# Sample state updates of a Gated DeltaNet kernel as rounded products on 96 stacked rows

## The chip, the cores and the metric

The kernel runs on one NeuronCore of a Trainium2 chip. The metric is the device time in microseconds of one launch, as the median of the runs. The matmul engine is called PE here, with PEld for its weight loads; DVE is the vector engine, ACT the scalar engine, POOL is GpSimd, SP issues the loads of the weights.

## The reference, cut to what matters

One inference step of one decoder layer: 256 prompt tokens and 8 sample sequences of 8 new tokens each (64 sample tokens), an input projection, eight MoBA attention heads, eight Gated DeltaNet heads, an output projection and a convolutional FFN. The change touches the last line of the delta rule, for the samples only:

```
def step(s, xs):
    ...
    u = lax.linalg.triangular_solve(lower, rhs, left_side=True, lower=True, unit_diagonal=True)
    qk = jnp.einsum('bhid,bhjd->bhij', qc, kc) * decay
    o = eg[..., None] * jnp.einsum('bhcd,bhde->bhce', qc, s) + jnp.einsum('bhij,bhje->bhie', qk, u)
    g_last = cg[..., -1]
    k_dec = kc * jnp.exp(g_last[..., None] - cg)[..., None]
    s_new = jnp.exp(g_last)[..., None, None] * s + jnp.einsum('bhcd,bhce->bhde', k_dec, u)
```

For a sample the chunk is its 8 tokens, so `s_new` of one sequence and one head is a 128x128 state plus a product over 8 rows: keys `k_dec` (8x128) against update rows `u` (8x128). There are 8 sequences and 8 heads.

## The kernel before

**Chunks.** All dense products stream their weights in chunks of 512x256 values (512 KB). The first 144 chunks (`NC1`) are the input projection (g0 and g1, the two groups of four DeltaNet heads, 32 chunks each; a0 and a1, the attention groups, 24 each) and the output projection; the FFN follows. For each chunk SP loads `w_raw`, ACT writes its rounded part `w_hi` (L821), DVE the rest `w_lo` (L1173), and PE runs 24 matmuls of 320 columns (L1774 to L1776: high by high, high by low, low by high). These products take fp32r operands, that is rounded ones, and are called rounded products here. The ring has four slots. PE waits at the head of chunk c for `w_lo` of chunk c (`products`). In chunk c ACT makes the high part of chunk c+3 first, DVE the low part of chunk c+2 first, and then each serves its other steps. DVE also takes the finished columns of every fourth chunk out of PSUM (`evac`) and, for g0 and g1, runs four taps of the convolution in the two chunks behind that (`conv`, L1223 and L1225: at quarter 1 and quarter 3 of each).

**Steps.** Everything else of the mixer is cut into steps, and `schedule()` lays them into the quarters of the chunks: `SLOTS[c, r]` is the list of steps behind quarter r of chunk c. PE serves its steps of a quarter behind that quarter's six matmuls; ACT and POOL serve all steps of a chunk in their order behind the chunk's first duty; DVE does, with the taps behind the steps of their quarter. Each engine works strictly in that order. `schedule()` counts in its own units: a step on PE moves the count `at` on by its `LENGTH` times 0.85 times `SPREAD`; a step elsewhere moves the due time `ready` of the next PE step by its `LENGTH` times `SPREAD` (1.4 for the delta rule). So the LENGTH of a step on ACT or DVE delays every later step of the chain.

**The sample unit.** `gdn_steps(g)` has units u = 0, 1 (prompt) and 2 (the 64 sample tokens). For unit 2: `kk` and `kq` (products of keys and queries), `tk` (PE turns the keys to token rows, DVE scales them into `tok_k`), `pl` and `dx` at levels 2 and 4 (the block inverse), `sh` (the state seen by keys and queries), `ks`, `u` (the update rows, ACT copies them to `u_tok`), `os`, `o`, `oc`, `oq`, `o1`, `or`, `o2`, `ot`, `oz` (the output). `ot` of the unit before sits behind `pl` at level 2, its `oz` on DVE behind that, and `sh` of head 0 waits for this `oz`. Then four times, once for each head: `um` (DVE, L1168 inside the helper: the 64 update rows times a mask, spread over four sequences, into `u_mask`), `us` on PE (L2057) and `us` on DVE (the decayed old state, then the sum, two operations on 128x1024), `so` (POOL stores the state). `um` 1 to 3 wait for the PE step `us` of the head before; `us` on PE waits for its `um`; `ot` waits for `o2` and for the last `us` on DVE.

PE's `us` before is two ordinary fp32 products, sequences 0 to 3 on rows 0 to 31 and sequences 4 to 7 on rows 32 to 63:

```
for i in range(2):
    ins = pe.matmul(psB[:, h % 2 * 2 + i, :], tk[32 * i:32 * i + 32, STATE_HEADS[h], :],
                    umask[32 * i:32 * i + 32, :, :].rearrange("p b e -> p (b e)"), start=True, stop=True)
```

**Where the steps lie before** (chunk, quarter). Group 0: `tk`, `pl` 2, `ot` of unit 1 at 40.2; `dx` 2 at 40.3; `sh` 0, `tv`, `pl` 4 at 41.1; `sh` 1, `dx` 4 at 41.3; `sh` 2, `sh` 3, `ks` at 42.1; `u` at 42.3; `os`, `o`, `oc`, `um` 0, `o1` at 43.0; `us` 0 to 3 at 44.0, 45.1, 46.2, 47.3; `ot` at 48.3. Group 1: `tk` and what follows at 72.3, `us` 0 to 3 at 76.1, 77.2, 78.3, 80.0; `ot` at 81.0.

Of the kernel before, what the change touches and what calls it, by code (L numbers as in the profile page):

```python
# [17 lines left out]
F32 = mybir.dt.float32  # L18
F32R = mybir.dt.float32r
I32 = mybir.dt.int32  # L20
ACT = mybir.ActivationFunctionType
ALU = mybir.AluOpType
AX = mybir.AxisListType

P = 128
# [3 lines left out]
NS = DB * DT  # L29
# [14 lines left out]
BLK = 32  # L44
# [133 lines left out]
STATE_HEADS = (1, 2, 3, 0)  # L178
# [7 lines left out]
def gdn_steps(g):  # L186
    decay = decay_steps((g, 0))
    s = decay[:1] + [("A", "qs", g, 0), ("P", "nr", g, 0), ("V", "ss", g, 0), ("G", "rn", g, 0)] + decay[1:]
    tail = []
    for u in (0, 1, 2):  # L190
        k, nxt = (g, u), (g, u + 1)
# [13 lines left out]
        s += tail[:1] + [("P", "tk", *k), ("V", "tk", *k)]  # L205
# [27 lines left out]
        s += [("P", "u", *k), ("A", "u", *k), ("P", "os", *k), ("A", "o", *k)]  # L233
# [9 lines left out]
        tail = [("V", "o2", *k), ("P", "ot", *k), ("V", "oz", *k)]  # L243
# [48 lines left out]
def ffn_param_steps():  # L292
    s = []
    for r in range(5):
# [156 lines left out]
def build(nc, I, O):  # L451
# [37 lines left out]
    work_at = m.at  # L489
    qn = m.put("q_squares", [P, 4, P])  # L490
    kb_at = m.at
    kb = m.put("k_squares", [P, 4, P])
    setat = m.at
# [3 lines left out]
    bv = m.put("tok_bv", [P, 4, P])  # L497
    qk = m.put("qk_t", [P, 4, P])
# [23 lines left out]
    umask = nc.alloc_sbuf_tensor_at("u_mask", [P, 4, P], F32, offset=setat + 4 * 2048)  # L522
# [64 lines left out]
    def C(name, n=P, m_=None):  # L587
        at, width = CONST_COLS[name]
        return cst[0:n, at:at + (width if m_ is None else m_)]
# [21 lines left out]
    def over_free(ap, count):  # L611

        return ap.unsqueeze(2).broadcast_to([ap.shape[0], ap.shape[1], count])

    def over_heads(ap, count):

        return ap.unsqueeze(1).broadcast_to([ap.shape[0], count, ap.shape[1]])
# [47 lines left out]
    def after(e, *key):  # L665

        e.wait_ge(done[key[0]], TALLY[key])
# [24 lines left out]
    root1 = cst[:, CONST_COLS["bucket"][0]:CONST_COLS["bucket"][0] + TOK]  # L692

# [43 lines left out]
    with block:  # L737
# [74 lines left out]
        def _(act):  # L812
            def finish(ins):
                ins.then_inc(done["A"], 1)
# [30 lines left out]
            def step(x):  # L845
# [74 lines left out]
                elif name == "u":  # L920
                    n = unit(k[1])[0]
                    after(act, "P", "u", *k)
                    finish(act.activation(ub[0:n].rearrange("p h d -> p (h d)"), b1[0:n], ACT.Copy))
                elif name == "o":
# [235 lines left out]
        def _(dve):  # L1160
            def finish(ins):
                ins.then_inc(done["V"], 1)
# [4 lines left out]
            def tt(out, a_, b_, op):  # L1167
                return dve.tensor_tensor(out, a_, b_, op)  # L1168
# [82 lines left out]
            def step(x):  # L1251
# [208 lines left out]
                elif name == "oz":  # L1460
# [6 lines left out]
                                                    op0=ALU.mult, op1=ALU.mult))  # L1467
                elif name == "um":
                    g, h = k
                    if h == 0:  # L1470
                        after(dve, "A", "o", g, 2)
                    else:
                        after(dve, "P", "us", g, h - 1)
                    finish(tt(umask[0:NS, :, :], over_heads(ub[0:NS, STATE_HEADS[h], :], 4), over_free(C("batch4", NS), P), ALU.mult))
# [287 lines left out]
        def _(pe):  # L1762
            def finish(ins):
                ins.then_inc(done["P"], 1)
# [61 lines left out]
            def step(x):  # L1826
# [225 lines left out]
                elif name == "us":  # L2052
# [3 lines left out]
                    for i in range(2):  # L2056
                        ins = pe.matmul(psB[:, h % 2 * 2 + i, :], tk[32 * i:32 * i + 32, STATE_HEADS[h], :],  # L2057
                                        umask[32 * i:32 * i + 32, :, :].rearrange("p b e -> p (b e)"), start=True, stop=True)
# [511 lines left out]
```

## Time and profile before

| | us |
|---|---|
| median of 3 runs | 1653.81 (1653.74 to 1655.29) |
| profiled execution | 1657.26 |
| its span, first to last instruction | 1655.6 |
| outside the span | 1.7 |
| PE busy | 1632.9 (99%) |
| DVE busy | 1050.5 (63%) |
| ACT busy | 617.3 (37%) |
| mean clock granted to PE | 0.996 of full speed |

Each line of the profile names the line of the kernel, the engine and the operation, the tiles written and read, the shapes, and a duration. Durations of PE overlap, since matmuls are pipelined: what a matmul costs is the time from its start to the start of the next. Those of DVE overlap by some 0.1 us.

### The profile page before, as it was taken

To read this page: it belongs to the slowest core of one execution; us is meant where nothing else is said; L and a number is where in the kernel's file an instruction comes from. 1 tells how busy PE (TensorE), PEld (TensorE's weight loads), DVE (VectorE), ACT (ScalarE), POOL (GpSimd) and SP (SyncE) were. 2 spreads that over 40 slices of the span, in tenths; PEclk is the share of its full clock that TensorE was granted. 3 is DMA by queue.
4 is the path that set the end of the run, shared out by engine and by line. 5 is a ranking of instruction groups with operands and counts; after the bars stand their busy time and mean duration, and the time that the engine had idled before them with its cause. 6 is when DMAs were issued, how large, how long until landed. Compare 5 with 4: busy or idle time off the path is not lost.

```text
span 1655.6 us, 30927 instructions
## 1 busy us (share of the span) xinstructions
PE 1632.9 (99%) x12899; PEld 1585.7 (96%) x12899; DVE 1050.5 (63%) x1716; ACT 617.3 (37%) x786; POOL 237.2 (14%) x370
## 2 busy tenths in 40 slices
PE   7999999999999999999999999999999999999997
PEld 7999989988998998999999999999999999999997
DVE  5676688656544455676666666666666666666665
ACT  6444323332343343643333333333333333333334
POOL 1121342123213022210000010101010101010004
PEclk9999999999999999999999999999999999999999
DMA  8453355344857467444544444444445444445442
GB/s 239 131 153 111 110 145 162 102 117 142 255 184 244 140 209 232 135 146 149 158 148 153 153 148 147 151 153 149 145 152 153 147 148 150 154 140 155 151 153 84
DMA packets 231243, 256.64 MB, mean 155 GB/s; under 512 B 9444, under 2 KB 220966, under 8 KB 231104
## 3 DMA queue, kind: packets, MB, share of 16 engines
q1 hardware_dynamic: 217856, 220.10, 43.2%
q0 software_dynamic: 10560, 33.29, 6.4%
q8 instruction: 102, 1.67, 0.4%
q10 hardware_dynamic: 2688, 1.27, 0.3%
q14 instruction: 37, 0.30, 0.1%
HBM read 243.50 MB, written 12.69 MB: 155 GB/s over the span
## 4 chain that ended last, share of the span: by engine, by line
PE 93%; DVE 3%; DMA 1%; issue 1%; ACT 1%; POOL 0%; SPq 0%; DVEq 0%; POOLq 0%; ACTq 0%
PE ps_proj L1774 22%; PE ps_proj L1775 21%; PE ps_proj L1776 21%; PE ps_small L1774 6%; PE ps_small L1776 6%; PE ps_small L1775 6%; PE ps_small L1816 2%; DMA w_raw<-in_w_in_dram 1%; PE ps_small L2048 0%; PE ps_small L1958 0%; PE ps_small L2136 0%; DVE w_lo L1173 0%; PE ps_small L1948 0%; PE ps_small L2154 0%; DMA state_s<-in_state_gdn_dram 0%
## 5 line engine op out<-in xcount | busy, mean ns | idle before, releaser
L1774 PE MATMUL ps_proj<-x_hi,w_hi 128*128 128x320 f32 x2432 | 766.2, 315 | 1.5 <-DVE x_lo L1290 1.0
L1776 PE MATMUL ps_proj<-x_hi,w_lo 128*128 128x320 f32 x2432 | 752.3, 309 | 0.0
L1775 PE MATMUL ps_proj<-x_lo,w_hi 128*128 128x320 f32 x2432 | 752.3, 309 | 0.0
L821 ACT ACTIVATE w_hi<-w_raw 128x1024 fp32r<-128x1024 f32 x408 | 432.1, 1059 | 741.4 <-PE ps_proj L1776 546.2
L1173 DVE TENSOR_TENSOR w_lo<-w_raw,w_hi 128x1024 fp32r<-128x1024 f32 x408 | 498.1, 1223 | 302.4 <-ACT w_hi L821 302.0
L1774 PEld LDWEIGHTS ps_proj<-x_hi,w_hi 128*128 128x128 f32 x2432 | 457.3, 188 | 15.0 <-issue 9.9
L1775 PEld LDWEIGHTS ps_proj<-x_lo,w_hi 128*128 128x128 f32 x2432 | 457.9, 188 | 0.2
L1776 PEld LDWEIGHTS ps_proj<-x_hi,w_lo 128*128 128x128 f32 x2432 | 457.4, 188 | 0.0
L1774 PE MATMUL ps_small<-hid_hi,w_hi 128*128 128x320 f32 x704 | 218.0, 310 | 0.0
L1776 PE MATMUL ps_small<-hid_hi,w_lo 128*128 128x320 f32 x704 | 217.6, 309 | 0.0
L1775 PE MATMUL ps_small<-hid_lo,w_hi 128*128 128x320 f32 x704 | 217.5, 309 | 0.0
L2514 POOL TENSOR_TENSOR ffn_ext<-ffn_params_t,consts 128x16 f32<-128x16 f32 x88 | 53.4, 628 | 800.4 <-DVE ffn_acc L1634 800.4
L1774 PEld LDWEIGHTS ps_small<-hid_hi,w_hi 128*128 128x128 f32 x704 | 132.1, 188 | 0.2 <-issue 0.2
L1775 PEld LDWEIGHTS ps_small<-hid_lo,w_hi 128*128 128x128 f32 x704 | 132.1, 188 | 0.0
L1776 PEld LDWEIGHTS ps_small<-hid_hi,w_lo 128*128 128x128 f32 x704 | 132.1, 188 | 0.0
L1168 DVE TENSOR_TENSOR x_res<-ps_small,x_res 128x640 f32<-128x640 f32 (+1 forms) x89 | 72.6, 815 | 49.6 <-PE ps_small L1776 49.6
L1634 DVE SCALAR_TENSOR_TENSOR ffn_acc<-ffn_ext,ffn_params_t,ffn_acc 128x336 f32<-128x336 f32 x176 | 94.3, 567 | 3.9
L1168 DVE TENSOR_TENSOR ffn_ext<-ps_proj,root 128x512 f32<-128x512 f32 x132 | 41.7, 372 | 0.0
L1774 PE MATMUL ps_proj<-gated_hi,w_hi 128*128 128x320 f32 x128 | 41.2, 322 | 0.0
L1776 PE MATMUL ps_proj<-gated_hi,w_lo 128*128 128x320 f32 x128 | 39.5, 309 | 0.0
L1775 PE MATMUL ps_proj<-gated_lo,w_hi 128*128 128x320 f32 x128 | 39.5, 309 | 0.0
L1225 DVE SCALAR_TENSOR_TENSOR conv_acc<-u_ext,params_t,conv_acc 128x344 f32<-128x344 f32 x72 | 38.3, 572 | 0.7
(351 smaller groups left out, 1217.0 us busy)
## 6 DMA issues: line engine op xcount, KB each, us to landing
w_raw<-in_w_up_dram SPq DMA_DIRECT2D x176, 512.0 KB, 3.5
w_raw<-in_w_in_dram SPq DMA_DIRECT2D x112, 512.0 KB, 3.8
w_raw<-in_w_down_dram SPq DMA_DIRECT2D x88, 512.0 KB, 3.5
w_raw<-in_w_out_dram SPq DMA_DIRECT2D x32, 512.0 KB, 4.1
k_pages<-in_cache_k_dram POOLq DMA_DIRECT2D x32, 256.0 KB, 3.4
v_pages<-in_cache_v_dram POOLq DMA_DIRECT2D x32, 256.0 KB, 4.3
state_s<-in_state_gdn_dram POOLq DMA_DIRECT2D x10, 512.0 KB, 5.5
out_ss_dram<-state_s POOLq DMA_DIRECT2D x8, 512.0 KB, 4.5
```

Source lines behind the costliest of these rows:

```text
L821: act.activation(whi[:, slot], raw[:, slot], ACT.Copy).then_inc(hi_done, 1)
L1168: return dve.tensor_tensor(out, a_, b_, op)
L1173: dve.tensor_tensor(wlo[:, slot], raw[:, slot], whi[:, slot].bitcast(F32), ALU.subtract).then_inc(lo_done, 1)
L1225: ins = dve.scalar_tensor_tensor(out=acc[:, j, 0:344], in0=u, scalar=wcol, in1=acc[:, j, 0:344], op0=ALU.mult, op1=ALU.add)
L1634: ins = dve.scalar_tensor_tensor(out=facc[:, kind, j, 0:336], in0=u, scalar=w_(tap), in1=facc[:, kind, j, 0:336], op0=ALU.mult, op1=ALU.add)
L1774: pe.matmul(o, hi, rhs_hi[:, k0 + kk_, :], start=first and kk_ == 0, stop=False)
L1775: pe.matmul(o, hi, rhs_lo[:, k0 + kk_, :], start=False, stop=False)
L1776: ins = pe.matmul(o, lo, rhs_hi[:, k0 + kk_, :], start=False, stop=last and kk_ == CQ - 1)
L1816: return pe.transpose(out, in_, C("ident", n, n))
L2514: ins = pool.tensor_tensor(fue[:, kind, j, 2 + SEQ:338].rearrange("p (b s) -> p b s", b=DB)[:, :, 0:2], old, C("ones", P, 16).rearrange("p ...
```

## The change

The keys and the update rows of the samples are split in a rounded high part and the rest, and stacked by rows, once for each half batch i (sequences 0 to 3 and 4 to 7). `tok_k_stack` i holds high, rest, high of the keys in three blocks of 32 rows (rest, high, high for i = 1), `u_stack` i high, high, rest of the update rows; `u_mask` becomes two tiles of 96 rows. One rounded product over 96 rows then gives high by high, rest by high and high by rest for a half batch. New steps: `th` (ACT, 4 copies of 32x512) and `tl` (DVE, 2 subtractions of 32x512) behind `tk` of unit 2; `uh` (ACT, 4 copies) and `ul` (DVE, 2 subtractions) between `os` on PE and `o` on ACT. `um` becomes two operations of 96x512 in place of one of 64x512. The planner's LENGTH of `us` on PE goes from 12 to 6, of `um` from 8 to 16; `th` and `uh` are entered with 20, `tl` and `ul` with 12.

```diff
@@ gdn_steps
-        s += tail[:1] + [("P", "tk", *k), ("V", "tk", *k)]
+        s += tail[:1] + [("P", "tk", *k), ("V", "tk", *k)] + ([("A", "th", g), ("V", "tl", g)] if u == 2 else [])
...
-        s += [("P", "u", *k), ("A", "u", *k), ("P", "os", *k), ("A", "o", *k)]
+        s += [("P", "u", *k), ("A", "u", *k), ("P", "os", *k)] + ([("A", "uh", g), ("V", "ul", g)] if u == 2 else []) + [("A", "o", *k)]
@@ scalar engine
+                elif name == "th":
+                    g = k[0]
+                    after(act, "V", "tk", g, 2)
+                    after(act, "P", "cg", g, 2)
+                    for i, rows in ((0, low32), (1, next32)):
+                        act.activation(tks[rows, i], tk[rows], ACT.Copy)
+                    for i, rows in ((0, low32), (1, next32)):
+                        ins = act.activation(tks[NS:NS + 32, i], tk[rows], ACT.Copy)
+                    finish(ins)
+                elif name == "uh":
+                    g = k[0]
+                    after(act, "A", "u", g, 2)
+                    for i, rows in ((0, low32), (1, next32)):
+                        act.activation(us_[i][rows], ub[rows], ACT.Copy)
+                    for i, rows, other in ((0, low32, next32), (1, next32, low32)):
+                        ins = act.activation(us_[i][other], ub[rows], ACT.Copy)
+                    finish(ins)
@@ vector engine
+                elif name == "tl":
+                    g = k[0]
+                    after(dve, "A", "th", g)
+                    tt(tks[next32, 0], tk[low32], tks[low32, 0].bitcast(F32), ALU.subtract)
+                    finish(tt(tks[low32, 1], tk[next32], tks[next32, 1].bitcast(F32), ALU.subtract))
+                elif name == "ul":
+                    g = k[0]
+                    after(dve, "A", "uh", g)
+                    for i, rows in ((0, low32), (1, next32)):
+                        ins = tt(us_[i][NS:NS + 32], ub[rows], us_[i][rows].bitcast(F32), ALU.subtract)
+                    finish(ins)
                 elif name == "um":
...
                         after(dve, "A", "o", g, 2)
+                        after(dve, "V", "ul", g)
...
-                    finish(tt(umask[0:NS, :, :], over_heads(ub[0:NS, STATE_HEADS[h], :], 4), over_free(C("batch4", NS), P), ALU.mult))
+                    for i in range(2):
+                        ins = tt(ums[0:NS + 32, i], over_heads(us_[i][0:NS + 32, STATE_HEADS[h], :].bitcast(F32), 4),
+                                 over_free(C("batch4", NS + 32), P), ALU.mult)
+                    finish(ins)
@@ tensor engine
                     for i in range(2):
-                        ins = pe.matmul(psB[:, h % 2 * 2 + i, :], tk[32 * i:32 * i + 32, STATE_HEADS[h], :],
-                                        umask[32 * i:32 * i + 32, :, :].rearrange("p b e -> p (b e)"), start=True, stop=True)
+                        ins = pe.matmul(psB[:, h % 2 * 2 + i, :], tks[0:NS + 32, i, STATE_HEADS[h], :],
+                                        ums[0:NS + 32, i].rearrange("p b e -> p (b e)"), start=True, stop=True)
```

The new tiles lie on memory that is free by then (`tok_k_stack` on the squares of q and k, the two `u_stack` on the decay tiles, `u_mask` on `qk_t` and `a_t`).

## Rows read from the trace of the kernel before

**Rows 1.** the page, busy time and its share of the span, instructions.
```profile
PE 1632.9 (99%) x12899; PEld 1585.7 (96%) x12899; DVE 1050.5 (63%) x1716; ACT 617.3 (37%) x786; POOL 237.2 (14%) x370
```

**Rows 2.** windows: stretch, length, PE, PEld, DVE, ACT, POOL busy, clock, DMA.
```profile
205.77:226.57 20.80, 19.45 (x295) 17.07 (x293) 16.60 (x34) 4.65 (x8) 9.61 (x14) 1.00 0.54 153
231.40:261.80 30.40, 30.31 (x190) 26.18 (x189) 29.58 (x44) 8.34 (x11) 12.63 (x17) 1.00 0.64 180
401.50:424.10 22.60, 22.60 (x138) 18.79 (x137) 20.07 (x22) 5.93 (x6) 5.66 (x5) 1.00 0.64 179
```

**Rows 3.** timeline of PE around one sample state update: start, length in us.
```profile
237.80 0.31 PE L1776 MATMUL ps_proj<-x_hi,w_lo 128*128 128x320 f32 x1
...
238.04 1.13 PE L2057 MATMUL ps_small<-u_mask,tok_k 32*128 32x512 f32 x4
...
239.09 0.41 PE L1774 MATMUL ps_proj<-x_hi,w_hi 128*128 128x320 f32 x1
...
239.34 0.31 PE L1775 MATMUL ps_proj<-x_lo,w_hi 128*128 128x320 f32 x1
```

**Rows 4.** timeline of PE, two rounded products of 512 columns.
```profile
307.66 0.31 PE L1776 MATMUL ps_proj<-x_hi,w_lo 128*128 128x320 f32 x1
...
307.80 0.39 PE L1921 MATMUL ps_small<-upto_g_hi,ones_r 128*128 128x512 f32 x1
...
308.26 0.31 PE L1774 MATMUL ps_proj<-x_hi,w_hi 128*128 128x320 f32 x1
```

**Rows 5.** timeline of PE, two rounded products on 64 rows.
```profile
179.92 0.31 PE L1776 MATMUL ps_proj<-x_hi,w_lo 128*128 128x320 f32 x1
...
180.16 0.38 PE L1921 MATMUL ps_small<-upto_g_hi,ones_r 64*128 64x256 f32 x1
...
180.59 0.41 PE L1774 MATMUL ps_proj<-x_hi,w_hi 128*128 128x320 f32 x1
```

**Rows 6.** tile ffn_rows: count, ns min/median/max, starts, form.
```profile
L1816 PE MATMUL ps_small<-consts,ffn_rows x20: 237/238/239, 679.8 to 695.5; 88*128 88x88 f32 x20
```

**Rows 7.** groups, DVE, 205 to 264 us: count, busy us, mean ns.
```profile
L1173 DVE TENSOR_TENSOR w_lo<-w_raw,w_hi 128x1024 fp32r<-128x1024 f32 x13 | 15.8, 1220 | 0.1
...
L1225 DVE SCALAR_TENSOR_TENSOR conv_acc<-u_ext,params_t,conv_acc 128x344 f32<-128x344 f32 x18 | 9.4, 563 | 0.1
...
L1168 DVE TENSOR_TENSOR state_s<-ps_small,state_s 128x1024 f32<-128x1024 f32 x4 | 4.9, 1224 | 0.1
...
L1168 DVE TENSOR_TENSOR u_mask<-u_tok,consts 64x512 f32<-64x512 f32 x4 | 2.8, 691 | 0.0
```

**Rows 8.** timeline of DVE in the same stretch.
```profile
212.07 0.67 DVE L1168 TENSOR_TENSOR tok_k<-ps_small,small 64x512 f32<-64x512 f32 x1
...
229.39 1.18 DVE L1433 SCALAR_TENSOR_TENSOR tok_bv<-ps_small,small,tok_bv 64x128 f32<-64x128 f32 x4 [3.38 <-ACT tok_bv L927]
...
253.53 0.69 DVE L1168 TENSOR_TENSOR tok_bv<-tok_bv,small 64x512 f32<-64x512 f32 x1
...
258.38 1.21 DVE L1173 TENSOR_TENSOR w_lo<-w_raw,w_hi 128x1024 fp32r<-128x1024 f32 x1
```

**Rows 9.** timeline of PE, at level 2 of the inverse.
```profile
210.36 0.44 PE L1948 MATMUL ps_small<-inv_blocks,a_t_levels 32*32 32x32 f32 x16 [1.35 <-POOL a_t_levels L2334]
```

**Rows 10.** timeline of PE, three starts of chunks 50, 51 and 52.
```profile
258.28 0.31 PE L1774 MATMUL ps_proj<-x_hi,w_hi 128*128 128x320 f32 x1
...
261.80 0.31 PE L1774 MATMUL ps_proj<-x_hi,w_hi 128*128 128x320 f32 x1
...
267.90 0.46 PE L1774 MATMUL ps_proj<-x_hi,w_hi 128*128 128x320 f32 x1
```

**Rows 11.** groups of ACT, 160 to 300 us.
```profile
L902 ACT ACTIVATE q_squares<-reg 128x512 f32<-128x512 f32 x2 | 1.2, 616 | 0.0
```

**Rows 12.** windows (columns as in rows 2), two stretches.
```profile
268.00:272.00 4.00, 4.00 (x22) 4.00 (x21) 3.27 (x7) 2.62 (x4) 0.61 (x1) 0.59 0.01 3
280.00:284.00 4.00, 4.00 (x54) 3.46 (x54) 3.71 (x9) 2.87 (x4) 2.90 (x3) 0.69 0.41 126
```

More of the change, by code:

```diff
@@ L489, in build @@
     work_at = m.at
+    qn_at = m.at
     qn = m.put("q_squares", [P, 4, P])
@@ L497, in build @@
     bv = m.put("tok_bv", [P, 4, P])
+    qk_at = m.at
     qk = m.put("qk_t", [P, 4, P])
@@ L521, in build @@
     upto_lo = [nc.alloc_sbuf_tensor_at(f"upto_g_lo{i}", [P, 4, P], F32R, offset=o) for i, o in ((0, kb_at), (1, tk_at))]
-    umask = nc.alloc_sbuf_tensor_at("u_mask", [P, 4, P], F32, offset=setat + 4 * 2048)
+    tks = nc.alloc_sbuf_tensor_at("tok_k_stack", [P, 2, 4, P], F32R, offset=qn_at)
+    us_ = [nc.alloc_sbuf_tensor_at(f"u_stack{i}", [P, 4, P], F32R, offset=o) for i, o in ((0, setat), (1, dec0_at))]
+    ums = nc.alloc_sbuf_tensor_at("u_mask", [P, 2, 4, P], F32R, offset=qk_at)
     w = Span(work_at)
@@ L692, in build @@
     root1 = cst[:, CONST_COLS["bucket"][0]:CONST_COLS["bucket"][0] + TOK]
+    low32, next32 = slice(0, BLK), slice(BLK, 2 * BLK)
     def decay(u):
```

6 rows, old and new, of the table LENGTH are left out of this document.

## The prediction

> **What bounds the kernel now.** I read the page first: PE is busy for 1632.9 us of a span of 1655.6, DVE for 63% of it [rows 1]. Taken over the whole, any PE time saved is time won, and DVE has room. Then I cut the span at the starts of chunks and asked again for the stretches in which the changed steps lie. In group 0, from the start of chunk 44 to that of chunk 51 (231.40 to 261.80), DVE is busy for 29.58 of 30.40 us, as full as PE. In group 1 the same steps fill DVE only for 20.07 of 22.60 us, and in group 0 from chunk 40 to 42 for 16.60 of 20.80 [rows 2]. The difference between the groups is the convolution and the evacuation into `u_ext`, which go on in group 0 while g1 is projected and are over in group 1. So PE sets the pace in both, but in group 0 DVE is next by a hair: it ends `w_lo` of chunk 51 at 258.38 + 1.21 = 259.59 [rows 8], and PE needs it at 261.80 [rows 10], 2.2 us later. This slack decides what the change is worth there.
>
> **The state update on PE.** Before: the last matmul ahead of the step starts at 237.80, the second behind it at 239.34, so 1.54 us, less two ordinary gaps of 0.147 (3.52 us for the 24 of a chunk [rows 10]): 1.25 us [rows 3]. The four records there overlap, two halves at a time. After: two rounded products of 512 columns. The nearest rows are those of `upto_g_hi` and the one behind it: 307.66 to 308.26 less one gap, 0.45 us [rows 4]. They are on 128 rows, the new ones on 96. On 64 rows, two products of 256 columns take from 179.92 to 180.59, and the matmul behind them is 0.1 longer [rows 5]: with the columns doubled about 0.83 us. I take 0.45, as the 88-row form is recorded under 88*128, not under a smaller tile as the 64-row one is [rows 6]; 0.83 stays as the upper bound. Saving: 0.80 us a step (bound 0.42), for eight steps 6.4 (3.4).
>
> One rule speaks against the change. The rows show two halves of 32 rows run at the same time [rows 3]. The Trainium skill ("TensorE: Matmul & The Clock Gate", Part 3, packing small matmuls) says that a product on 32 rows takes as long as one on 128 and that the gain of small tiles is this concurrency, which the 96 stacked rows give up. By its gap for 512 columns, about 216 ns each, the two products one after the other would come to an estimated 0.43 us. The rows give 0.45, so the trace agrees: the fp32 form lost more than the concurrency gave.
>
> **New work.** `th` and `uh`: four copies each on ACT, nearest row 0.616 us for 512 elements a row [rows 11], at 0.53 pitch 2.2 us. Bounds: 4 x 0.2 (if 32 rows were cheap) and 4 x 0.62. `tl` and `ul`: two subtractions each on DVE; `um`: one more operation per head. All have 512 elements a row, as the 64-row `u_mask` has: 0.69 us [rows 7], some 0.62 in pitch. That is 1.25 us for each of `tl` and `ul` and 0.62 for each `um`: 5.0 us of DVE for each group. Bounds 4 and 5.5.
>
> **Where the planner puts it.** I worked the planner's sum through with the new lengths. In group 0 `tk` stays at 40.2; `pl` 2 and `ot` go from 40.2 to 41.3, `dx` 2 to 42.0, `sh` 0, `tv`, `pl` 4 to 42.2, `sh` 1, `dx` 4 to 43.0, `sh` 2, 3 to 43.2, `u` to 44.0, `os` with `uh`, `ul`, `o`, `oc`, `um` 0 to 44.1; `us` to 46.2, 48.0, 49.2, 51.0, 1.5 chunks apart where it was 1.25; `ot` to 52.0. The first steps of group 1 move by one chunk. In group 1: `us` to 78.3, 80.1, 81.3, 83.1, `ot` to 84.1; the first attention group meets its old place at 90.0. No load of SP or store of POOL is added; those behind `us` move with it, `hk` too.
>
> **Group 0, first part.** What goes: PE's wait of 1.35 us for POOL's mask at `pl` 2 [rows 9], as `pl` comes 3 us later. What comes: DVE ends `tok_k` at 212.07 + 0.6 = 212.7 [rows 8]; now it waits for `th`, to 215.0, then `tl` to 216.25. Behind it on DVE stand tap 1 (1.0), `w_lo` 43 (1.15), tap 2 (1.0), `oz` (0.66), tap 3 (1.0), `w_lo` 44 (1.15), `dx` 2 (0.55): `oz` ends at 220.1, `dx` 2 at 222.8. On ACT the high part of chunk 44 and `pl` 2 stand behind `th`: 216.2. PE, from 205.77: its steps keep their cost, 7.7 us in all (20.80 [rows 2] less three chunks of 3.52, the wait of 1.4 and some 1.2 for `u`), of which `tk` 0.4, `pl` with `ot` 1.0, `sh` 1.0 a head. So chunk 41 starts at 209.7, 42 at 214.2; `dx` 2 waits for ACT from 215.1 to 216.3, `sh` 0 for `oz` from 218.7 to 220.2, `pl` 4 for DVE's `dx` 2 from 221.7 to 222.9. That is 3.9 us of new waits against 1.4 lost. Chunk 44 starts at 205.77 + 4 x 3.52 + 7.7 + 3.9 = 231.4, `u` is done at 233.4, `uh` at 236.15.
>
> **Group 0, second part.** From `ul` on DVE has no gap. Before, it takes from 229.39 (`oc`) to 254.2 (`o2`) [rows 8]: 24.8 us, 0.4 of them idle. After, the same list has also four operations of `um` (2.5), three more `w_lo` (3.45: chunks 51 to 53, since the updates lie further apart) and four more taps (0.73 + 3 x 0.98 = 3.7; a tap pair is 2 x 0.563 by [rows 7], less overlap): 34.0, and ahead of it `ul`, 1.25. From 236.2 that ends at 271.4. PE would be at `ot` at 260.9 if nothing held it. On the way it waits for `um` 3 (1.4), for `w_lo` 52 (1.5) and at `ot` for `o2` (3.2), beside small ones. `ot` ends at 271.9. Before, PE has done the same chunks and steps at 261.80 + 3.52 + 0.88 = 266.2 [rows 10]. Group 0: 5.7 us later; its own saving of 3.2 is within this.
>
> **Group 1.** No taps, and DVE idles. The same walk, with the stretch of 22.60 us filled to 20.07 [rows 2] and no chunk's part late: `oz` is done 1.2 us before PE comes to `sh` 0, `um` 0 3.5 us before its `us`; each later `um`, `w_lo` and `o2` is ready ahead of PE (closest `o2`, 0.2 us). So 4 x 0.80 = 3.2 us are won. DVE's wait for `bias_q` moves and leaves 1 us of slack.
>
> **Sum.** + 5.7 - 3.2 = + 2.5 us against the profiled execution: 1657.26 + 2.5 = 1659.8. The median of the runs is 3.45 lower than that execution. In it PE's clock is at its lower level, 1.2 GHz, in two stretches, 0.59 and 0.69 of full in four us each [rows 12], each costing some 1.2 to 1.5 us (a matmul of 0.46 in place of 0.31 us [rows 10]); I put most of the 3.45 on this. The sum on the median: 1656.3. The new waits leave PE idle ahead of just the steps behind which it fell before, so I add half of such a stretch, 0.7: 1657.0.
>
> **The rivals.** (A) The PE saving comes out whole: DVE's extra work fits into its room of 37% [rows 1]. Then 8 x 0.80 + 1.4 = 7.8 us less, 1646.0; part of it gives up to 1650.5. Against it: 29.58 of 30.40 [rows 2]. Chance 0.12. (B) The front chain is shorter than I walked it (cheap 32-row copies, `oz` early): up to 3.9 us back, 1651 to 1654.5. Chance 0.15. (C) Slower: clock. In 262 to 271 PE idles for more than 6 us in three pieces. If it falls to 1.2 GHz there and again behind the one-column products that follow, two stretches more, 2.7 us on top of 1656.3, and if the 96 rows cost 0.83, 1.5 more in group 1: 1659 to 1661. It decides from the point where PE's idle share before `ot` brings the clock down. The Trainium skill ("TensorE: Matmul & The Clock Gate", Part 1) says that PE, once idle, goes to half its rate and must be busy again before it recovers; in this trace the clock fell behind the one-column products, with PE recorded busy. Chance 0.25. (D) The update isn't on the rounded path or the planner puts nothing elsewhere: can't be, both stand in the diff.
>
> **How the numbers follow.** The forecast (1654.5 to 1659, DVE bound in group 0) has 0.48. Range: from 1651.5 (most of B) to 1661.0 (C). A measurement of this kernel can tell some 0.2%, 3.3 us, from no change, so faster is below 1650.5 and slower above 1657.1. Faster: A, 0.12. Slower: C, 0.25, and some 0.4 of the forecast, 0.20: 0.45. Same: 0.43.
>
> **What would show it.** `us` on PE: two records 0.22 apart, 0.45 in all; 0.8 refutes the step. DVE without a gap from `ul` to `o2` in group 0, some 35 us, and PE's waits with `um`, `w_lo` and `tok_bv` as releasers, up to 3 us at `ot`; if `ot` starts before 265, the ledger of DVE is wrong. `dx` 2, `sh` 0 and `pl` 4 waiting 1 to 1.5 us each. Group 1 without waits, 3.2 us shorter. The clock below full around 268 to 275.

## The result and the profile after

The changed kernel takes 1662.21 us (median of 9 runs, 1660.01 to 1667.29) against 1655.29 beside it: a ratio of 1.0045 with a 95% interval of 1.0035 to 1.0054. It is slower by 6.9 us, on the side that the prediction gave the most chance, but 1.2 us above the end of its range and 5.2 above its number. Its runs fall into two groups, six of 1660.01 to 1662.52 and three of 1666.66 to 1667.29, which are called short and long here. The profiled execution is a short one: 1660.69 us, span 1659.0, against 1657.26 before, so only 3.4 us of the 6.9 lie between the two profiled executions.

First line of the page of after, as [rows 1]:

```profile
PE 1626.5 (98%) x12883; PEld 1585.2 (96%) x12883; DVE 1059.2 (64%) x1732; ACT 626.8 (38%) x802; POOL 236.4 (14%) x370
```

PE has 6.4 us less to do, as much as eight steps by 0.80, and the kernel is longer: the time went into waits. (The cleanest part of this is group 1, at the full clock in both, below: 82.26 and 79.18 us of PE, 3.1 less, 0.77 a step.) DVE has 8.7 us more, ACT 9.5.

Windows of before, cut at the starts of chunks 40, 44 and 52, and 72 to 90 for group 1 (stretch, length, then PE, PEld, DVE, ACT and POOL busy, clock, DMA):

```profile
205.77:231.41 25.64, 24.29 (x327) 21.54 (x325) 18.55 (x40) 7.41 (x12) 9.61 (x14) 1.00 0.51 145
231.41:267.90 36.49, 36.33 (x232) 31.84 (x231) 34.14 (x53) 12.44 (x17) 15.22 (x19) 1.00 0.65 187
...
377.26:459.52 82.26, 82.26 (x714) 75.02 (x713) 48.70 (x67) 24.35 (x29) 21.32 (x33) 1.00 0.69 208
```

The same chunks of after:

```profile
205.34:231.50 26.16, 22.02 (x302) 19.94 (x301) 17.73 (x36) 8.00 (x13) 9.57 (x14) 1.00 0.49 142
231.50:267.87 36.37, 33.62 (x226) 31.23 (x225) 32.97 (x54) 13.82 (x21) 11.59 (x17) 1.00 0.47 135
...
381.83:462.13 80.30, 79.18 (x707) 75.33 (x705) 53.33 (x75) 28.09 (x35) 18.68 (x28) 1.00 0.67 203
```

Group 1 is 1.96 us shorter. In group 0 `ot` and the last `us` fall behind other chunks than before, so its balance is drawn later, at chunk 60: from chunk 40 to there it is 306.93 - 205.77 = 101.16 us before and 311.48 - 205.34 = 106.14 after, 5.0 longer. Another 0.8 comes at chunk 127, where PE waits 0.9 us for `k_pages` that it found loaded before. 5.0 - 2.0 + 0.8, and 0.4 that after is ahead at chunk 40, give the 3.4 of the two executions.

The waits of PE in after, 205 to 285 us, which is group 0 (line, releaser, us in total, times, the longest), and below them the new one of group 1, with the line of DVE that stands ahead of its `o2`:

```profile
PE ps_small L2073 <- DVE tok_bv L1191: 3.1, 1, 3.1
PE ps_small L2086 <- DVE z_gate L1489: 1.7, 1, 1.7
PE ps_small L1996 <- ACT prod_blocks L918: 1.4, 1, 1.4
PE ps_small L2095 <- DVE u_mask L1191: 1.3, 2, 1.0
PE ps_proj L1812 <- DVE w_lo L1196: 1.2, 1, 1.2
PE ps_small L1986 <- DVE inv_t_blocks L1272: 1.0, 1, 1.0
```

```profile
PE ps_small L2073 <- DVE tok_bv L1191: 1.1, 1, 1.1
```

```profile
435.86 1.23 DVE L1191 TENSOR_TENSOR state_s<-state_s,small 128x1024 f32<-128x1024 f32 x1 [1.14 <-DMA state_s<-in_state_gdn_dram]
```

L2073 is `ot` waiting for `o2`, L2086 `sh` 0 for `oz`, L1996 `dx` 2 for ACT's `pl`, L1986 `pl` 4 for DVE's `dx` 2. The two before `ot`, the mask and `w_lo`, lie at 263.3 and 267.9.

In group 1 DVE itself is idle for 1.14 us, until the old state of the last head is loaded, and its three operations behind that end with `o2`. PE's wait of 1.1 has the length of this idle time. The same idle time, 1.0 to 1.2 us, is in e5, e6, e9, e11, e12, e13 and e15, and not in before and e2.

One state update on PE, to be held against [rows 3] (timeline: start, length):

```profile
243.43 0.31 PE L1814 MATMUL ps_proj<-x_hi,w_lo 128*128 128x320 f32 x1
243.58 0.62 PE L2095 MATMUL ps_small<-u_mask,tok_k_stack 96*128 96x512 f32 x2
244.03 0.31 PE L1812 MATMUL ps_proj<-x_hi,w_hi 128*128 128x320 f32 x1
```

From 243.43 to 244.03 is 0.60, less a gap of 0.147: 0.45 us. The new operations on ACT and DVE in group 0, and DVE's queue up to `o2`:

```profile
212.37 1.27 ACT L935 ACTIVATE tok_k_stack<-tok_k 32x512 fp32r<-32x512 f32 x2 [5.71 <-DVE tok_k L1191]
213.65 1.27 ACT L937 ACTIVATE tok_k_stack<-tok_k 32x512 fp32r<-32x512 f32 x2
```

```profile
236.79 1.38 DVE L1191 TENSOR_TENSOR u_stack<-u_tok,u_stack 32x512 fp32r<-32x512 f32 x2 [3.02 <-ACT u_stack L945]
...
261.94 1.28 DVE L1191 TENSOR_TENSOR u_mask<-u_stack,consts 96x512 fp32r<-96x512 f32 x2
...
266.50 2.40 DVE L1196 TENSOR_TENSOR w_lo<-w_raw,w_hi 128x1024 fp32r<-128x1024 f32 x2
...
271.37 0.69 DVE L1191 TENSOR_TENSOR tok_bv<-tok_bv,small 64x512 f32<-64x512 f32 x1
```

A 32-row operation takes what one of 64 or 128 rows takes (0.63 on ACT, 0.69 on DVE). DVE has no gap from 236.79 to 272.06.

### The profile page after: what moved, and what is told of

Its sections match the earlier page's. It is cut to its first block, busy times and chain, and to the rows that moved or that the text cites. A ratio compares the mean times of both kernels' runs of the same rounds, so it can differ in the third digit from the quotient of the medians.

```text
span 1659.0 us, 30931 instructions
## 1 busy us (share of the span) xinstructions
PE 1626.5 (98%) x12883; PEld 1585.2 (96%) x12883; DVE 1059.2 (64%) x1732; ACT 626.8 (38%) x802; POOL 236.4 (14%) x370
## 4 chain that ended last, share of the span: by engine, by line
PE 92%; DVE 4%; DMA 1%; issue 1%; ACT 1%; POOL 0%; SPq 0%; DVEq 0%; POOLq 0%; ACTq 0%
PE ps_proj L1812 22%; PE ps_proj L1813 21%; PE ps_proj L1814 21%; PE ps_small L1812 6%; PE ps_small L1813 6%; PE ps_small L1814 6%; PE ps_small L1854 2%; DVE w_lo L1196 1%; DVE state_s L1191 1%; DVE conv_acc L1248 1%; DMA x_raw<-in_x_sample_dram 0%; PE ps_proj L1854 0%; PE ps_small L2174 0%; PE ps_small L2192 0%; PE ps_small L1996 0%
```

## The experiments

All stand beside runs of the kernel before on the same chip. The clock is the mean granted to PE in an execution, as a share of full speed. "From chunk 40 to 60" is group 0 and what overlaps it, "from chunk 72 to 90" group 1, both taken from the traces.

| kernel | median us (runs) | ratio, 95% | clock of its runs |
|---|---|---|---|
| the change | 1662.21 (9) | 1.0045, 1.0035 to 1.0054 | 0.993 to 0.998 |
| e1 old places | 1674.59 (4) | 1.0116, 1.0099 to 1.0133 | 0.990 to 0.992 |
| e2 places alone | 1652.99 (10) | 0.9986, 0.9977 to 0.9996 | 0.996 to 0.999 |
| e3 no rest | 1666.29 (4) | 1.0066, 1.0050 to 1.0083 | 0.993 to 0.994 |
| e4 split alone | 1668.09 (4) | 1.0078, 1.0061 to 1.0095 | 0.993 to 0.996 |
| e5 the change again | 1667.44 (4) | 1.0065, 1.0048 to 1.0082 | 0.992 to 0.994 |
| e6 product, late | 1661.02 (9) | 1.0028, 1.0017 to 1.0039 | 0.992 to 0.996 |
| e7 reordered | 1659.46 (10) | 1.0021, 1.0012 to 1.0031 | 0.994 to 0.997 |
| e8 reordered, masks on POOL | 1659.01 (10) | 1.0021, 1.0012 to 1.0031 | 0.995 to 0.997 |
| e9 `ot` later | 1660.60 (8) | 1.0029, 1.0018 to 1.0039 | 0.996 to 0.998 |
| e10 before, one wait | 1660.28 (10) | 1.0025, 1.0015 to 1.0034 | 0.995 to 0.998 |
| e11 second group alone | 1651.73 (7) | 0.9973, 0.9961 to 0.9984 | 0.996 to 0.999 |
| e12 the same, `ot` later | 1651.34 (7) | 0.9970, 0.9959 to 0.9982 | 0.997 to 0.999 |
| e13 short taps | 1660.26 (10) | 1.0028, 1.0014 to 1.0042 | 0.992 to 0.998 |
| e14 before, more waits | 1662.42 (8) | 1.0040, 1.0028 to 1.0052 | 0.994 to 0.996 |
| e15 the change, third time | 1661.37 (10) | 1.0044, 1.0028 to 1.0061 | 0.992 to 0.998 |

**e1, the operations without the places.** The planner's lengths are those of before, so every step stands where it stood:

```diff
-"us": 6
+"us": 12
-"th": 20, "uh": 20
+"th": 1 / 1.4, "uh": 1 / 1.4
-"um": 16, "tl": 12, "ul": 12
+"um": 8, "tl": 1 / 1.4, "ul": 1 / 1.4
```

> The changed kernel with the planner's lengths chosen so that every step lies where it lay before (us 12, um 8, the four new steps 0); all new operations stay. Theory (group 0 is bound by DVE, the loss is made by the new DVE and ACT operations standing in its queue, and by the later places only in part): DVE needs 5.0 us more between tok_k and the last state sum of group 0, its slack before was 2.2 us, and pl, dx and sh now come 1 to 2 us behind a tok_k_stack that is not ready, so group 0 is 2 to 5 us longer than before, group 1 0 to 3 us shorter; in all 0 to +4 us on the kernel before. Rival (the later places alone make the loss): as fast as the saving on PE says, 6 us less than before. Rival (TensorE's clock makes it): the dip-free stage tables of before and this one agree, and only the granted clock differs.

18.9 us slower, far more than expected, and in both groups: from chunk 40 to 60 it takes 110.44 us, before 101.16, and from chunk 72 to 90 it takes 89.64 for 82.26. So group 1 has room for the new operations only at the change's places; at the old ones it loses 7.4 us. Part of both is the clock (0.990 to 0.992). The waits of PE in group 0 (the last line is also in before, [rows 9]):

```profile
PE ps_small L2095 <- DVE u_mask L1191: 3.4, 2, 2.2
PE ps_small L1996 <- ACT prod_blocks L918: 3.4, 1, 3.4
PE ps_small L2073 <- DVE tok_bv L1191: 2.4, 1, 2.4
PE ps_small L1986 <- POOL a_t_levels L2372: 1.3, 1, 1.3
```

**e2, the places without the operations.** The planner's sum is that of the change; then the split steps are left out and the mask and the products are those of before:

```diff
+    for at_ in slots:
+        slots[at_] = [x for x in slots[at_] if x[1] not in ("th", "tl", "uh", "ul")]
```

> The kernel before with its steps laid where the change lays them, and none of the new operations (fp32 products of 32 rows, one u_mask operation per head). Theory: DVE has no more work of its own, but the updates lie 1.5 chunks apart, over the taps of the next pair; the wait of 1.35 us for POOL's mask goes. Group 0 0 to 2 us longer, group 1 the same: -1 to +2 us on before. Rival (the places make the loss): +4 to +7 us.

2.7 us faster (just outside no change), with one wait of 0.2 us in group 0. So the places gain and the operations lose: with the old operations the places are worth 2.7 us, with the new ones 18.9 - 6.9 = 12 (from two comparisons).

**e3 and e4, which of the operations.** Both at the old places. e3 writes high parts only (two 96-row copies for `th` and `uh`, no `tl`, `ul`), with the new masks and products; e4 has all four split steps but the old masks and products:

```diff
 e3
-                    for i, rows in ((0, low32), (1, next32)):
-                        act.activation(tks[rows, i], tk[rows], ACT.Copy)
-                    for i, rows in ((0, low32), (1, next32)):
-                        ins = act.activation(tks[NS:NS + 32, i], tk[rows], ACT.Copy)
+                    for i in range(2):
+                        ins = act.activation(tks[0:NS + 32, i], tk[0:NS + 32], ACT.Copy)
 e4
-                        ins = pe.matmul(psB[:, h % 2 * 2 + i, :], tks[0:NS + 32, i, STATE_HEADS[h], :],
+                        ins = pe.matmul(psB[:, h % 2 * 2 + i, :], tk[32 * i:32 * i + 32, STATE_HEADS[h], :],
```

> At the old places; th and uh are two copies of 96 rows each, tl and ul are left out, so the rests of keys and update rows are not formed and the third block holds stale rows: the states of the samples are wrong. The new products and the doubled u_mask stay. Theory: DVE has 2.5 us more per group, ACT half the copies. us on PE costs 0.45 us each against 1.25, 6.4 us in all; group 1 gets its 3.2, group 0 some 0 to 3 of them: 3 to 6 us less than before. Rival (the product on 96 rows costs 0.8 us): 1 to 3 us less.

> At the old places; th, tl, uh, ul run and their stacks are read by nobody, the products and u_mask are those of before. This prices the splitting alone. Theory: 2.5 us of DVE and 5 us of ACT for each group, with DVE's waits for th and uh (2.3 us and 2 us) in its queue: +3 to +6 us on before, most of it in group 0 where PE waits at dx, sh and pl. Rival (DVE has room of 37%, so it is hidden): within 1 us of before.

e3 is 10.6 us slower than before, e4 12.4, where 3 to 6 us less and 3 to 6 more were expected. Each part of the new work costs more at the old places than the whole change costs at its own (6.9). The split steps cost at `dx` 2, where ACT's `pl` stands behind them (3.4 us in e4, 1.9 in e3); the doubled masks at `ot`, where PE waits 6.2 us in e3, over both groups, and 0.4 in e4. At `us` it waits alike, 2.5 and 2.4.

**e5 and e15, the change again.**

> The changed kernel once more, for a second trace. Theory 1 (DVE's queue sets the time of group 0 and the rest of the difference is the clock): again about 1.0045 of before; if this profiled execution is a long one (some 1667 us), its trace has one or two more stretches at the lower clock than the first, each at 1.2 to 1.7 us, and the same waits around the state updates. Rival: the long ones come from a late transfer or a wait of another place; then the chunk starts part from the first trace's at one point where PE waits for DMA, at an unchanged clock.

> The change once more, on the chip of e13 and e14. Theory 1: a mixture of 1660 to 1662.5 and 1664 to 1668, the longer ones with the lower mean clock, ratio 1.004 to 1.007. Rival (which of the two it is goes by the chip): all of one kind.

e5 had four runs, all long (1664.38 to 1667.60); e15 had, on one chip, six of 1658.65 to 1661.38 at clocks of 0.996 to 0.998 and four of 1665.07 to 1668.71 at 0.992 and 0.993. So it doesn't go by the chip. With the nine of the first comparison, 11 of 23 executions of the change are long, and none of some 90 of before went over 1660.4. The waits of PE in e5, 205 to 290 us, are the six lines of after, number for number. What differs are the windows behind `ot`, of after and then of e5:

```profile
268.00:276.00 8.00, 4.87 (x24) 4.49 (x25) 7.90 (x13) 3.87 (x5) 3.51 (x6) 0.79 0.92 264
276.00:284.00 8.00, 8.00 (x63) 7.90 (x62) 5.79 (x16) 2.62 (x4) 1.03 (x1) 1.00 0.13 44
```

```profile
268.00:276.00 8.00, 4.39 (x20) 4.04 (x21) 7.90 (x12) 4.48 (x7) 3.64 (x7) 0.73 0.91 268
276.00:284.00 8.00, 8.00 (x34) 7.81 (x33) 3.79 (x12) 1.34 (x2) 1.51 (x2) 0.50 0.18 60
284.00:292.00 8.00, 8.00 (x56) 8.00 (x55) 7.21 (x17) 3.62 (x5) 0.46 (x1) 0.92 0.22 69
```

Twice the missing share of the clock times the length gives the time at 1.2 GHz: 3.4 us in after, 13.6 in e5 (and 3.4 more near 300). From chunk 40 to 60, e5 takes 111.87 us and after 106.14: 5.7 us for 13.6 more slow ones, 0.42 each. PE comes out of its wait at `ot` at the lower clock; its timeline in after:

```profile
272.12 0.64 PE L2073 MATMUL ps_small<-consts,tok_bv 64*128 64x64 f32 x4 [3.13 <-DVE tok_bv L1191]
...
275.25 0.47 PE L1812 MATMUL ps_proj<-x_hi,w_hi 128*128 128x320 f32 x1
...
275.72 0.31 PE L1814 MATMUL ps_proj<-x_hi,w_lo 128*128 128x320 f32 x1
275.86 0.28 PE L1933 MATMUL ps_small<-consts,q_squares 128*128 128x1 f32 x2
```

In after, the matmuls (0.47 us) are back to 0.31 just ahead of the one-column products of group 1 (L1933); in e5 PE goes through these, and what follows, at 1.2 GHz.

**e6, the products at their own places, without the subtractions.**

```diff
+        slots[at_] = [x for x in slots[at_] if x[1] not in ("tl", "ul")]
```

(and the copies of e3, at the change's places.)

> The change at its own places, but the high parts are written by two ACT copies of 96 rows each and the low parts' subtractions tl and ul are left out, so the state updates are those of high parts only, counted thrice. It stands against the steps at the same places with the old products (1652.99). Theory 1: without tl and ul the front chain is shorter by some 2.5 us of DVE and 2 x 1 us of ACT, the masks stay on DVE, and the new products save 0.8 us each in group 1 (3.2) and some of it in group 0: 1648 to 1651. Rival (the product is no cheaper for the kernel wherever DVE or the planner's places decide): 1652 to 1655.

1661.02: outside both ranges. The front is as expected: chunk 44 comes 22.05 us behind chunk 40, in the change 26.16, in e2 22.04. So `tl` and the doubled copies cost 4.1 us there and the high parts alone nothing. At chunk 52 the lead over the change is 6.0 us (56.52 behind chunk 40 for 62.53), although the wait at `ot`, still to come, is the same:

```profile
PE ps_small L2070 <- DVE tok_bv L1189: 3.1, 1, 3.1
PE ps_proj L1809 <- DVE w_lo L1194: 1.2, 1, 1.2
PE ps_small L2092 <- DVE u_mask L1189: 0.4, 1, 0.4
```

At chunk 60 the lead is only 2.1 (104.02 for 106.14): behind `ot` this execution has 13.6 us at 1.2 GHz, after 3.4, and eight of nine runs have the clock of the long executions, 0.992 to 0.994. That the wait at `ot` is the same fits the ledger of the prediction: from `oc` to `o2` DVE has the same list in both kernels, again without a gap, and takes 33.9 us in both (233.27 to 267.14, in after 238.20 to 272.06).

**e7 and e8, another order.** `th` stands behind the last `dx`, `tl` behind `ks`, `uh` behind `o`, `ul` ahead of the first mask; e8 has the masks on POOL as well:

```diff
-        s += tail[:1] + [("P", "tk", *k), ("V", "tk", *k)] + ([("A", "th", g), ("V", "tl", g)] if u == 2 else [])
+        s += tail[:1] + [("P", "tk", *k), ("V", "tk", *k)]
-            s += [("V", "ks", *k)]
+            s += [("A", "th", g), ("V", "ks", *k), ("V", "tl", g)]
-            s += [("V", "um", g, 0)]
+            s += [("V", "ul", g), ("V", "um", g, 0)]
 e8
-            s += [("V", "ul", g), ("V", "um", g, 0)]
+            s += [("V", "ul", g), ("G", "um", g, 0)]
```

> All work of the change, but th stands behind the last dx, tl behind ks, uh behind o and ul behind oc, so that nothing of the triangular solve waits behind them on ACT or DVE. Theory 1: the front's three new waits of 3.9 us go, DVE's sum from ul to o2 stays, so the part before chunk 44 is some 3 us shorter and part of it is given back at ot: 1655 to 1660, PE still waiting for u_mask and tok_bv. Rival (the chain of the split operations is what costs, wherever it stands): no gain over the change, 1661 to 1666.

> As the reordered one, with the masks um on POOL: 0.62 x 8 = 5 us less on DVE in each group. Theory 1: DVE's stretch from ul to o2 shortens from 35 to 30 us, PE's waits for tok_bv go; if a mask on POOL takes under 2.5 us a head it is ready ahead of its us: 1649 to 1655. Rival (the masks are as slow on POOL that us waits for them, 4 to 8 times by 1 to 3 us): 1660 to 1670.

(The planner's LENGTH of `th` and `tl` is next to nothing in both, so the front stands at its old places again, with POOL's wait of 1.3 us, and `ot` at 50.3.) e7 came into its range: the three front waits are gone, and the one at `ot` is 4.8 us. e8 missed its range by 4 us. DVE has the masks no more, but look at its timeline and POOL's (e8):

```profile
234.48 2.03 DVE L1196 TENSOR_TENSOR w_lo<-w_raw,w_hi 128x1024 fp32r<-128x1024 f32 x1
...
240.05 2.06 DVE L1196 TENSOR_TENSOR w_lo<-w_raw,w_hi 128x1024 fp32r<-128x1024 f32 x1
...
246.49 1.22 DVE L1196 TENSOR_TENSOR w_lo<-w_raw,w_hi 128x1024 fp32r<-128x1024 f32 x1
```

```profile
233.38 2.03 POOL L2370 TENSOR_TENSOR u_mask<-u_stack,consts 96x512 fp32r<-96x512 f32 x2 [10.63 <-DVE u_stack L1191]
...
238.39 2.63 POOL L2370 TENSOR_TENSOR u_mask<-u_stack,consts 96x512 fp32r<-96x512 f32 x2
```

While POOL works on a mask, DVE's `w_lo` takes 2.03 us in place of 1.22, and taps are longer by as much. From `ul` to `o2` DVE has the same list in e7 and e8 but for the eight operations of the masks, 5.2 us; it takes 33.1 us in e7 and 32.4 in e8. So nearly all that was taken from DVE came back in its other operations (six `w_lo` 9.7 us for 7.2, the taps 8.4 for 6.7), and PE waits 2.0 us for POOL's masks besides.

**e9, `ot` of group 0 one chunk later.**

```diff
+    if x == ("P", "ot", 0, 2):
+        return 53
```

> The change with the last transposes ot of group 0, and what stands behind them, one chunk later (53.0 for 52.0), so that DVE's o2 is done when PE comes. Theory 1 (the wait of 3.1 us at ot is both time and what brings the clock down in the executions near 1667): the wait goes, no execution lies above 1664, the clock's mean is 0.996 or more in nearly all, median 1657 to 1659.5. Rival (DVE's debt only moves on, to w_lo): PE waits as much for w_lo of chunks 53 to 55, times as the change's, 1660 to 1667.

The wait is gone and so are the long executions: eight runs, 1659.54 to 1662.99, none under 0.996. (The traced one is the longest of them; it has 6.8 us at 1.2 GHz behind the wait below, and 3.4 more near 295.) The median fell less than expected, as a wait of 2.3 us for `upto_g_lo`, which is behind the same queue of DVE, took the place of the 3.1:

```profile
PE ps_small L1961 <- DVE upto_g_lo L1193: 2.3, 1, 2.3
```

Each theory had one half: without the wait at `ot` there are no long executions, and DVE's debt moves on.

**e10 and e14, waits put into the kernel before.** Five more masks ahead of `o2` of group 0, and in e14 four more ahead of the mask of its last head:

```diff
+                    if k == (0, 2):
+                        for _ in range(5):
+                            chain(tt(umask[0:NS, :, :], over_heads(ub[0:NS, STATE_HEADS[0], :], 4), over_free(C("batch4", NS), P), ALU.mult))
```

> The kernel before with five more operations on DVE (the last mask once more, its result unread) ahead of o2 of group 0, 3.2 us: PE, which comes to ot just as o2 ends, waits 3 us there. Theory 1: the loss is larger than the wait: 3 us and 2 to 7 more from a longer stretch at 1.2 GHz behind it, 1660 to 1665. Rival (a wait costs its length): 1658 to 1659.5 and the same clock as before.

> The kernel before with nine more operations on DVE (the last mask written again, its result unread): four ahead of the mask of the last head of group 0, five ahead of its o2; 5.9 us, so that PE waits in two or three pieces within ten us, about as in the change. Theory 1: the waits cost their 5.5 to 6 us in every execution, and some or most executions have the long stretch: 1661 at the shortest, up to 1668, clock down to 0.993, median 1662 to 1667. Rival (waits cost their length alone, as one wait of 3.8 did): 1660.5 to 1662.5, clock as before.

PE's waits, in e10 and then in e14:

```profile
PE ps_small L2038 <- DVE tok_bv L1168: 3.8, 1, 3.8
```

```profile
PE ps_small L2041 <- DVE tok_bv L1168: 5.3, 1, 5.3
...
PE ps_small L2063 <- DVE u_mask L1168: 0.6, 1, 0.6
```

The medians grew by 4.5 us for 3.8 of wait and by 7.3 for 5.9, within about 1.5 us of the waits' own length, and no execution was over 1664.3. In the traces, from chunk 40 to 60, it is 3.2 and 5.2 us over before, with 6.8 us at 1.2 GHz behind the wait in both and as much, in two stretches, in before [rows 12]. So a wait here costs about its length. The claim that such a wait as such brings the stretch of 13.6 us has fallen. In these kernels `ot` stands behind chunk 48, 2.75 chunks ahead of the one-column products; in the change and e6 half a chunk.

**e13, the changed kernel with work taken from DVE.** Taps 1 to 3 in chunks 44 to 51 are cut to 8 columns of 344:

```diff
-                            conv(n, tap // 2)
+                            conv(n, tap // 2, 8 if 44 <= c <= 51 else 344)
```

> The change, with taps 1 to 3 of the convolution that DVE does from chunk 44 to 51 (beside the state updates of group 0) cut to 8 columns of 344, so some channels of group 1's convolution are wrong. It takes 7 to 9 us of work from DVE there and nothing from PE. Theory 1 (DVE's queue is the bound from ul to o2, and its waits bring the long stretch at the lower clock): PE's waits for u_mask, w_lo and tok_bv there (5.6 us) go, the three waits of the front (4.1) stay, no execution above 1660, clock 0.996 or more: 1654 to 1657.5. Rival 1 (the clock falls without them): times up to 1662 with clocks of 0.993. Rival 2 (PE waits on something else that DVE's waits only hide, the state's loads or ACT): less than 3 us gained.

The median is 1660.26, 1.1 us under the change beside it (e15), so theory 1 missed its range. Here are the wait at `ot`, DVE from `ul` to `o2`, and PE at `ot`:

```profile
PE ps_small L2074 <- DVE tok_bv L1191: 3.0, 1, 3.0
```

```profile
237.01 1.38 DVE L1191 TENSOR_TENSOR u_stack<-u_tok,u_stack 32x512 fp32r<-32x512 f32 x2 [3.02 <-ACT u_stack L945]
...
258.65 1.28 DVE L1191 TENSOR_TENSOR u_mask<-u_stack,consts 96x512 fp32r<-96x512 f32 x2
...
267.38 0.69 DVE L1191 TENSOR_TENSOR tok_bv<-tok_bv,small 64x512 f32<-64x512 f32 x1
```

```profile
268.13 0.46 PE L2074 MATMUL ps_small<-consts,tok_bv 64*128 64x64 f32 x4 [2.96 <-DVE tok_bv L1191]
```

The edit took less from DVE than expected: from `ul` to `o2` it needs 31.1 us (237.01 to 268.07) where the change needs 35.3, 4.2 less in place of 7 to 9, and again it has no gap. `ot` starts sooner by just that: 62.57 us behind chunk 40 for 66.78, 4.2. So the first half of theory 1 holds: DVE's queue from `ul` to `o2` sets when `ot` runs. Why, then, is the wait at `ot` as long as before? The masks and `w_lo` hold PE no more, and it comes to `ot` 33.45 us behind chunk 44. `o2` lets it go on at 36.4: the wait of 3.0. In the change `ot` runs 40.6 us behind chunk 44, 7.2 more than PE needs when nothing holds it. It waits these 7.2 us in pieces, on the way and at `ot`, and the 4.2 taken from DVE removed the pieces on the way. The last would have gone with 3.0 us more. This is worked out from the two traces; no run took so much.

The second half of theory 1, the clock, missed. Chunk 52 starts 58.57 us behind chunk 40 (in the change 62.53), but chunk 60 106.64 (106.14): between them this execution has 13.7 us at 1.2 GHz, after 3.4, and 10.3 more at 0.42 each are 4.3, all that had been gained. Five of ten runs lie above 1660.7, at 0.992 to 0.995. Rival 2 has its number (less than 3 us gained), but not its reason.

**e11 and e12, the change in group 1 alone.** Group 0 has the old products, masks and no split steps, at the change's places:

```diff
+        slots[at_] = [x for x in slots[at_] if x[1] not in ("th", "tl", "uh", "ul") or x[2]]
```

> The change in group 1 alone: group 0 keeps the old products, one mask a head and no th, tl, uh, ul, at the change's places. Theory 1 (DVE is full in group 0, idles in group 1): group 0 as with the places alone (1652.99), group 1 some 2 us shorter as in the change: 1649.5 to 1652, faster than before by 0.2% or more. Rival (the new products gain nothing that the places did not give): 1653 to 1655.

> As e11, with ot of group 1 half a chunk later (84.3 for 84.1), where in the change PE waited 1.1 us for o2. Theory 1: that wait goes, 0.5 to 1.1 us less than e11: 1648.5 to 1651.5. Rival (behind it the pages of the first attention group arrive late and take it back): as e11.

e11 is faster than before by 4.1 us, 0.27%, with all runs between 1651.05 and 1652.23, and better than both kernels. Against e2 it gains in group 1 what the change gained there: 80.17 us from chunk 72 to 90, for 82.27 in e2. In group 0, chunk 40 to 60, it takes 96.5 us and the change 106.1: what the new operations cost at these places. e12 removed the wait at `ot` of group 1 and got another in its place (1.0 us for `w_lo`, behind the same idle time of DVE, 1.2 us for the load of the state), so its 0.4 us can't be told from none:

```profile
PE ps_proj L1823 <- DVE w_lo L1203: 1.0, 1, 1.0
```

## Why the prediction was right and where it was wrong

**Right, with their sizes.** The update on PE: 0.45 us forecast, 0.45 measured. The Trainium skill ("TensorE: Matmul & The Clock Gate", Part 3) speaks for the concurrency of small tiles that was given up; the trace agrees with the estimate of 0.43 that the prediction worked out from its gap for 512 columns. DVE as the thing that takes the gain in group 0: e11, where leaving group 0 alone turned a loss of 0.45% into a gain of 0.27%, and e13, where 4.2 us less on DVE brought `ot` 4.2 us sooner. The front chain: waits of 1.41, 1.74 and 1.00 us where 1.2, 1.5 and 1.2 were forecast, and chunk 44 at 231.50 for 231.4. The last mask, `w_lo` and `ot`: 1.0, 1.2 and 3.1 for 1.4, 1.5 and 3.2. DVE's stretch from `ul` to `o2`: 35.3 us for 35.2. Rivals A and B are out: nothing of the front came back. ACT's four copies took 2.54 us, not 2.2, which covers the 0.25 by which the front waits were longer.

**A slip without effect.** "PE would be at `ot` at 260.9 if nothing held it" leaves out steps that PE has on the way. From 231.4 the 33.45 us of e13 lead to 264.9, and the prediction's own waits taken off its 271.4 to 265.3. The sum doesn't use the 260.9.

**Mis-sized: group 1.** 3.2 us forecast, 1.96 measured. The step that failed is that each `o2` "is ready ahead of PE (closest `o2`, 0.2 us)": PE waits 1.1 us there. The loads of the states were put at nothing ("those behind `us` move with it"). But DVE idles 1.14 us until the last one has come (435.86 above); without this, `o2` would be done just as PE comes to `ot`. No run moved this load, so it is read from the trace and not tested.

**Missed: a transfer behind.** PE waits 0.9 us for `k_pages` at chunk 127 in after (0.3 in e15's trace). The text said that attention meets its old place at chunk 90 and looked no further. That the change brings this wait is not shown: e10 and e14, at the places of before, have it too, 0.7 and 0.6 us.

**Failed: the sum on the median.** The walk gave 1659.8 for the profiled execution, which took 1660.69, so it was 0.9 us short. Then 3.45 us were taken off to come to the median, and 0.7 added for the clock, which gave 1657.0. The change's median lies 1.5 us above its profiled execution, not 2.8 below: 0.9 + 3.45 - 0.7 + 1.5 are the 5.2 us. The failed step is this offset with its clock term. The prediction took the 3.45 us between before's profiled execution and its median as two slow stretches, which is about right (two of 3.4 us at 0.42 are 2.9), and then took the same 3.45 off the change. But the change's own short stretch, the one that starts as PE leaves the wait at `ot`, is there in all three of its traces (in e5 as the start of the long one), so it can't be taken off. At mean clocks of 0.997 and 0.998, 53 runs of before have a median of 1655.1 and nine of the change 1660.5: 5.4 us. The terms give this: group 0 is 5.0 longer in the traces, and 1.4 more as before's trace has one stretch more; less 1.96, and 0.8 for the pages: 5.2. On top of it 11 of 23 executions are longer by 6 to 7 us. Half of a stretch, 0.7 us, was the term for all this; it should have been 1.4 in every execution and 6 in every second one. Rival C named the mechanism (the clock, from the wait before `ot` and the one-column products behind it) and priced it at 2.7 us. The 13.6 us of e5 at 0.42 are 5.7, the 3.4 near 300 another 1.4, so this was too little by more than half.

**What stays open.** Why one execution leaves the lower clock after 3.4 us and another, with the same waits to a tenth of a microsecond, after 13.6. The traces hold more than these two: behind the wait ahead of or at `ot` PE has 3.4 us at 1.2 GHz in after, e8 and e15, 6.8 in e7, e10 and e14, 10.2 in e13 and 13.6 in e5 and e6. Nor does the clock fall at one point of the wait: in after as it ends, in e13 1.3 us behind its end, in e6 1.8 us ahead of it. The longer stretches, of 10.2 and 13.6, were seen where a wait of 3.0 or 3.1 us at `ot` ends half a chunk ahead of the one-column products (the change, e6, e13), and not where the wait was moved or missing at the same places (e9, e2, e11) nor behind longer waits 2.75 chunks ahead of those products (e10, e14); e7, with 4.8 us three quarters of a chunk ahead, lies between (clocks from 0.994). That the two must meet is argued from this, not shown: no run moved the one-column products by themselves, and most kernels have one trace. The Trainium skill ("TensorE: Matmul & The Clock Gate", Part 1) says that an idle PE loses half its rate and has to be busy again to recover. The first half this trace shows at 272.12; e5, busy in every window after 276 and at 0.50 up to 284, shows that being recorded as busy is not enough.

## What to carry to other kernels

Cheaper work on the bound engine is worth what the engine next to it has free in that very stretch: the same edit lost 5 us where DVE was full and won 2 where it had gaps, and doing it in the second place alone beat both kernels. The free time belongs to the schedule too: at the old places the second group lost 7.4 us. A wait is the last piece of a debt, not the whole of it: when work is taken from a full engine, the earlier waits of the other one go first, and the last stays until the rest is paid. So compare the times at which a step runs, not the waits ahead of it. Where an engine is late, look whether it was itself idle just before, for a load. And a median is compared with a median: an offset between one profiled execution and its median belongs to that kernel's waits and clock, and is not carried over to a kernel with other waits.

## What the runs showed that was not expected

- The same program with the same waits has executions 6 to 7 us apart, about evenly often; the traces of one of each kind differ by 13.6 us at 1.2 GHz, at 0.42 us each.
- DVE's subtraction of 128x1024 takes 1.22 us alone and 2.03 us while POOL multiplies a mask of 96x512; taking 5.2 us of masks from DVE to POOL shortened DVE's stretch by 0.7.
- The places alone were worth 2.7 us to the old operations and 12 us to the new ones: they take POOL's wait of 1.3 us at level 2 away [rows 9] and give the queues a quarter of a chunk more for each head.
